# Modulation sums by block transposes and row sums on VectorE, folded by four small products, in place of TensorE transposes

## The reference

```python
c_act = jax.nn.silu(c)                       # 1 x 1024
for l in range(2):
    mod = c_act @ w_ada[l] + b_ada[l]        # 1 x 6144
    sh1, sc1, g1, sh2, sc2, g2 = jnp.split(mod, 6, axis=-1)
    h = rmsnorm(x, norm1[l]) * (1.0 + sc1) + sh1
    ...                                      # retention, pooling, gates from h @ w_in[l]
    x = x + g1 * (merged @ w_out[l])
    h2 = rmsnorm(x, norm2[l]) * (1.0 + sc2) + sh2
    gate, up = jnp.split(h2 @ w_ffn_in[l], 2, axis=-1)
    x = x + g2 * ((jax.nn.silu(gate) * up) @ w_ffn_out[l])
```

## Time and profile before

| | |
|---|---|
| median of 3 runs | 1407.83 us (1406.99 to 1409.58) |
| the profiled execution, its own time | 1406.93 us |
| its span, first to last instruction | 1405.1 us |
| TensorE (PE), matmuls | 1388.5 us busy, 99% |
| TensorE, weight loads (PEld) | 1306.0 us, 93% |
| VectorE (DVE) | 1117.1 us, 79% |
| ScalarE (ACT) | 845.7 us, 60% |
| GpSimd (POOL) | 101.3 us, 7% |
| mean granted TensorE clock | 0.998 |
| DMA, mean | 214 GB/s |

### The profile page before, as it was taken

The page is one execution under the profiler, slowest core; times in us unless marked ns, Lnnn a source line. Parts: engine busy times, 40 slices in busy tenths (PEclk is TensorE's granted clock), DMA queues, the critical chain, the costliest instruction groups (busy, mean ns, idle before and its releaser), DMA issues.

```text
span 1405.1 us, 25824 instructions
## 1 busy us (share of the span) xinstructions
PE 1388.5 (99%) x10437; PEld 1306.0 (93%) x10437; DVE 1117.1 (79%) x1690; ACT 845.7 (60%) x1307; POOL 101.3 (7%) x157
## 2 busy tenths in 40 slices
PE   8999999999999999999999999999999999999998
PEld 7898888899889888899999999998999999999987
DVE  7898988889898888888777788777677777876653
ACT  6776776345776875347576575554465764754452
POOL 2000111100000011103100000000031000000000
PEclk9999999999999999999999999999999999999999
DMA  9643999986545999979954588887699555777662
GB/s 256 171 143 97 285 272 277 297 226 179 145 137 157 299 267 288 299 205 257 312 150 147 172 239 237 242 246 219 181 265 305 150 151 179 237 217 229 189 184 72
DMA packets 472981, 301.34 MB, mean 214 GB/s; under 512 B 15116, under 2 KB 454416, under 8 KB 472736
## 3 DMA queue, kind: packets, MB, share of 16 engines
q1 hardware_dynamic: 455344, 239.57, 61.0%
q0 software_dynamic: 16704, 58.29, 12.7%
q10 hardware_dynamic: 816, 1.84, 0.4%
HBM read 289.43 MB, written 1.05 MB: 207 GB/s over the span
## 4 chain that ended last, share of the span: by engine, by line
PE 89%; DVE 6%; ACT 2%; issue 2%; DMA 1%; SPq 0%; ACTq 0%; DVEq 0%
PE acc L2107 14%; PE acc L2108 14%; PE acc L2109 14%; PE mx L2124 11%; PE mx L2125 6%; PE acc L2124 6%; PE acc L2125 3%; DVE w_lo L1180 2%; PE mx L2108 2%; PE mx L2107 2%; PE mx L2109 2%; DVE ada_acc L1270 1%; PE acc L2152 1%; PE acc L2154 1%; PE acc L2153 1%
## 5 line engine op out<-in xcount | busy, mean ns | idle before, releaser
L1180 DVE TENSOR_TENSOR w_lo<-raw,w_hi 128x1024 fp32r<-128x1024 f32 x450 | 542.8, 1220 | 127.4 <-ACT w_hi L591 125.0
L591 ACT ACTIVATE w_hi<-raw 128x1024 fp32r<-128x1024 f32 x450 | 465.3, 1052 | 137.4 <-DMA raw<-in_w_in 61.9
L2107 PE MATMUL acc<-h,w_hi 128*128 128x256 f32 (+1 forms) x1472 | 421.5, 286 | 2.9 <-DVE w_lo L1180 2.5
L2108 PE MATMUL acc<-h,w_hi 128*128 128x256 f32 (+1 forms) x1472 | 412.9, 280 | 0.0
L2109 PE MATMUL acc<-h,w_lo 128*128 128x256 f32 (+1 forms) x1472 | 411.5, 280 | 0.0
L2107 PEld LDWEIGHTS acc<-h,w_hi 128*128 128x128 f32 x1472 | 277.4, 188 | 9.0 <-issue 3.7
L2108 PEld LDWEIGHTS acc<-h,w_hi 128*128 128x128 f32 x1472 | 277.5, 189 | 2.6 <-issue 2.4
L2109 PEld LDWEIGHTS acc<-h,w_lo 128*128 128x128 f32 x1472 | 277.9, 189 | 0.0
L2124 PE MATMUL mx<-u,w_hi 128*128 128x512 f32 x756 | 264.4, 392 | 0.0
L2125 PE MATMUL mx<-u,w_lo 128*128 128x256 f32 x756 | 213.1, 282 | 0.0
L2124 PEld LDWEIGHTS mx<-u,w_hi 128*128 128x128 f32 x756 | 141.9, 188 | 29.2
(11 more groups left out here) (334 smaller groups left out, 2288.1 us busy)
## 6 DMA issues: line engine op xcount, KB each, us to landing
raw<-in_w_in SPq DMA_DIRECT2D x132, 512.0 KB, 4.2
ada<-in_w_ada POOLq DMA_DIRECT2D x96, 512.0 KB, 5.8
raw<-in_w_ffn_in SPq DMA_DIRECT2D x88, 512.0 KB, 4.5
raw<-in_w_up SPq DMA_DIRECT2D x64, 512.0 KB, 5.5
raw<-in_w_down SPq DMA_DIRECT2D x64, 512.0 KB, 5.8
raw<-in_w_out SPq DMA_DIRECT2D x32, 512.0 KB, 4.0
raw<-in_w_ffn_out SPq DMA_DIRECT2D x32, 512.0 KB, 4.1
raw<-in_w_ret_o SPq DMA_DIRECT2D x16, 512.0 KB, 4.1
```

Of the source, the lines that this page charges most:

```text
L591: nc.scalar.activation(w_hi[:, n % NS], raw[:, n % NS], ACT.Copy).then_inc(hi_ready, 1)
L1180: V.tensor_tensor(w_lo[:, n % NS], raw[:, n % NS], w_hi[:, n % NS].bitcast(F32), ALU.subtract).then_inc(lo_ready, 1)
L2107: mm(outp, w_hi[:, i % NS, k], rhs[:, k, 0], start=k == 0, stop=False)
L2108: mm(outp, w_hi[:, i % NS, k], rhs[:, k, 1], start=False, stop=False)
```

## The change

- The four TensorE transposes per group go, and with them `ada_part` and VectorE's row sum and bias add per group.
- A group's products now all go to the first half of `ada_acc`. Right behind the last of them VectorE transposes that half in blocks of 32x32 into the second half (`ada_turned`), and sums each block's rows: 128x512 become 128x16 in `ada_rows`. So partition 32a+k holds, for piece n of 128 columns and block m, the sum over the 32 partitions of block a for column 128n+32m+k.
- The sum over the four values of a is left. `ada_fold` (128x32, four identities of 32 one above the other) does it on TensorE: `ada_sums(n)` is now four products, one per m, each with 32 output partitions and 4 columns per group, for all groups of one place at once. The places (`ADA_FOLDS`, first group and count): groups 0 to 6 beside slab 8 of layer 1's up projection, 7 to 15 in the first retention stage where the transposes of group 15 stood, 16 to 21 in the second retention stage where those of group 21 stood, 22 and 23 beside slab 39 of the last FFN stage. `ada_columns(n)` is one add of the bias there. The groups of layer 0's MLP stage are folded only in the MLP stage of layer 1.
- `ada_fold` is made by one row sum on VectorE in `rest_of_vectors`, at the start.
- A product that starts a group now waits for the row sum of the group before (`ada_row`); `ada_turned` waits for its products and, from the second fold's groups on, for the fold before. `ADA_DONE` and the wait in `whole_tiles` follow.
- The loads stay on POOL's queue, in the same order with the same waits.

```diff
@@ -119,14 +119,10 @@
     return beside
 
 
-def ada_sums_at(stage, later):
-
-    g0, n, at = ADA_PLAN[stage]
-    return {at(8 * i + 7) + later: g0 + i for i in range(n)}
-
-
-
-ADA_DONE = (0, 0, 7, 7, 14, 16, 20, 22, 24)
+
+ADA_FOLDS = ((0, 7), (7, 9), (16, 6), (22, 2))
+FOLD_A, FOLD_F = 8, 39
+ADA_DONE = (0, 0, 0, 0, 7, 16, 16, 22, 24)
 
 
 TILE_NORMS = (2, 4, 5, 6, 7, 8)
@@ -247,13 +243,14 @@
         negsink = sb("negsink", [P, 12])
         cact = sb("cact", [P, KT])
         head_eps = sb("head_eps", [P, 1])
-        ada_part = sb("ada_part", [P, 4])
+        ada_fold = sb("ada_fold", [P, 32])
+        ada_rows = sb("ada_rows", [P, 9, 4, 4])
         few = sb("few", [P, 16])
         mean_eps = sb("mean_eps", [P, 1])
         wgrp = sb("wgrp", [P, LAYERS * 4, P])
 
 
-        sb("before_u2", [P, 32])
+        sb("before_u2", [P, 116])
         with ExitStack() as mlp:
             u2 = sb("u2", [P, MLP_UP, 2, S], F32R, mlp)
             ru = sb("ru", [P, 2, 2 * S], F32, mlp)
@@ -938,7 +935,8 @@
                 def whole_tiles(*tiles):
                     for k in tiles:
                         if k == 0:
-                            act.wait_ge(ada_out, (14, 20)[l])
+                            act.wait_ge(ada_row, (14, 20)[l])
+                            act.wait_ge(ada_out, (7, 16)[l])
                         normed_high(h_norm, 2 * l, k, [t.rearrange("p (c t) -> p c t", c=2) for t in (sqb, rb)], y2,
                                     nx_of(l), lambda k: mod_of(l, k))
 
@@ -1252,15 +1250,15 @@
 
                 e, part = divmod(q, 2)
                 g, k = divmod(q, 8)
-                o = ada_acc[:, g % 2]
+                o = ada_acc[:, 0]
                 if q == 0:
                     dve.wait_ge(c_silu, 1)
                 if part == 0:
                     dve.wait_ge(ada_landed[e % 3], 16 * (e // 3) + 16)
                 w = cact[:, k:k + 1]
                 if k == 0:
-                    if g >= 2:
-                        dve.wait_ge(ada_col, g - 1)
+                    if g >= 1:
+                        dve.wait_ge(ada_row, g)
                     ins = V.tensor_scalar(o, ada[:, e % 3, 0], w, None, ALU.mult)
                 else:
                     if part == 0:
@@ -1273,20 +1271,34 @@
                 else:
                     ca.done(ins)
 
-            def ada_columns(g):
-                dve.wait_ge(ada_col, g + 1)
-                ca.link(V.tensor_reduce(ada_part[:], mx[:, 0].rearrange("p (n k) -> p n k", n=4), AX, ALU.add))
-                V.tensor_tensor(modT[:, 4 * g:4 * g + 4], ada_part[:], vecT[:, V_BADA + 4 * g:V_BADA + 4 * g + 4],
-                                ALU.add).then_inc(ada_out, 1)
+            def ada_turned(g):
+
+                n = [at <= g < at + count for at, count in ADA_FOLDS].index(True)
+                dve.wait_ge(ada_sum, ADA_UNITS * (g + 1))
+                if n:
+                    dve.wait_ge(ada_col, n)
+                ca.link(V.transpose(ada_acc[:, 1], ada_acc[:, 0]))
+                V.tensor_reduce(ada_rows[:, g - ADA_FOLDS[n][0]].rearrange("p n m -> p (n m)"),
+                                ada_acc[:, 1].rearrange("p (b k) -> p b k", b=16), AX, ALU.add).then_inc(ada_row, 1)
+
+            def ada_columns(n):
+                at, count = ADA_FOLDS[n]
+                dve.wait_ge(ada_col, n + 1)
+                V.tensor_tensor(modT[:, 4 * at:4 * (at + count)], mx[:, 0, 0:4 * count],
+                                vecT[:, V_BADA + 4 * at:V_BADA + 4 * (at + count)], ALU.add).then_inc(ada_out, count)
 
             def beside(stage):
-                tiles, columns = ada_tiles(stage), ada_sums_at(stage, 6)
+                tiles = ada_tiles(stage)
 
                 def work(p):
                     for q in tiles.get(p, ()):
                         ada_product(q)
-                    if p in columns:
-                        ada_columns(columns[p])
+                        if q % 8 == 7:
+                            ada_turned(q // 8)
+                    if (*stage, p) == ("A", 1, FOLD_A + 2):
+                        ada_columns(0)
+                    if (*stage, p) == ("F", 1, FOLD_F + 2):
+                        ada_columns(3)
                 return work
 
             def scaled_pair(counts, n, b):
@@ -1321,6 +1333,7 @@
 
             def rest_of_vectors():
                 dve.wait_ge(boot_t, 6)
+                boot.done(V.tensor_reduce(ada_fold[:], ident.rearrange("p (a k) -> p k a", a=4), AX, ALU.add))
                 boot.done(V.tensor_scalar(vecT[:, V_LN2:V_C], acc[:, 3, V_LN2:V_C], float(D) ** 0.5, None, ALU.mult))
                 V.tensor_copy(vecT[:, V_C:P], acc[:, 3, V_C:P]).then_inc(vec_ready, 1)
                 boot.done(V.tensor_copy(vecT[:, P:V_MLN], acc[:, 3, P:V_MLN]))
@@ -1875,13 +1888,13 @@
                 lo_upto(p0 + 25)
                 ada_product(8 * g0 + 7)
                 lo_upto(p0 + 26)
+                ada_turned(g0)
                 ada_product(8 * g0 + 8)
                 ada_product(8 * g0 + 9)
                 lo_upto(p0 + 28)
                 ada_product(8 * g0 + 10)
                 ada_product(8 * g0 + 11)
                 lo_upto(p0 + 29)
-                ada_columns(g0 + 0)
                 ada_product(8 * g0 + 12)
                 lo_upto(p0 + 30)
                 ada_product(8 * g0 + 13)
@@ -1892,11 +1905,12 @@
                 pooled(0)
                 lo_upto(p0 + 32)
                 ada_product(8 * g0 + 15)
+                ada_turned(g0 + 1)
                 lo_upto(p0 + 33)
                 gated(0)
                 pooled(1)
                 lo_upto(p0 + 35)
-                ada_columns(g0 + 1)
+                ada_columns(1 + l)
                 gated_low(0)
                 pooled(2)
                 lo_upto(p0 + 36)
@@ -2164,12 +2178,12 @@
                     mm(mx[:, 0, 0:S], one, ssq[:, 0], start=True, stop=False)
                     mm(mx[:, 0, 0:S], one, ssq[:, 1], start=False, stop=True).then_inc(n_ss, 1)
 
-            def ada_sums(g):
-                pe.wait_ge(ada_sum, ADA_UNITS * (g + 1))
-                if g >= 1:
-                    pe.wait_ge(ada_out, g)
-                for n in range(4):
-                    ins = nc.tensor.transpose(mx[:, 0, n * P:(n + 1) * P], ada_acc[:, g % 2, n * P:(n + 1) * P], ident)
+            def ada_sums(n):
+
+                at, count = ADA_FOLDS[n]
+                pe.wait_ge(ada_row, at + count)
+                for m in range(4):
+                    ins = mm(mx[32 * m:32 * (m + 1), 0, 0:4 * count], ada_fold[:], ada_rows[:, 0:count, :, m], start=True, stop=True)
                 ins.then_inc(ada_col, 1)
 
             h_part = lambda k: hd2[:, k]
@@ -2488,11 +2502,9 @@
                 norm_sum(l * 2 + 1)
                 up_slab(2)
                 up_slab(3)
-                sums = ada_sums_at(("A", l), 4)
-
                 def ada_after(p):
-                    if p in sums:
-                        ada_sums(sums[p])
+                    if (l, p) == (1, FOLD_A):
+                        ada_sums(0)
 
                 pe.wait_ge(n_var, l * 2 + 2)
                 for k in range(MLP_UP):
@@ -2640,19 +2652,16 @@
                 pe.wait_ge(b_vsb, l * 4 + 1)
                 values2(2)
                 project(22, 23, 24)
-                pe.wait_ge(b_p, l * 8 + 1)
-                ada_sums(g0 + 0)
                 project(25)
                 pe.wait_ge(b_vsb, l * 4 + 3)
                 ret_outputs(0)
-                pe.wait_ge(ada_out, g0 + 1)
                 ret_scores(1)
                 project(26)
                 pe.wait_ge(b_vsb, l * 4 + 2)
                 ret_sums(0)
                 project(27, 28, 29, 30)
                 pe.wait_ge(b_p, l * 8 + 3)
-                ada_sums(g0 + 1)
+                ada_sums(1 + l)
                 pe.wait_ge(b_gt, l * 4 + 1)
                 ret_outputs(1)
                 project(31)
@@ -2708,11 +2717,9 @@
                 out_slab(6)
                 out_slab(7)
 
-                sums = ada_sums_at(("F", l), 4)
-
                 def ada_after(p):
-                    if p in sums:
-                        ada_sums(sums[p])
+                    if (l, p) == (1, FOLD_F):
+                        ada_sums(3)
 
                 for s in range(FFN_IN):
                     if s < 4:
```

More of the change, by code:

```diff
@@ L357, in program @@
         ada_landed = [sem(f"ada_landed{j}") for j in range(3)]
-        ada_sum = sem("ada_sum"); ada_col = sem("ada_col"); ada_out = sem("ada_out")
+        ada_sum = sem("ada_sum"); ada_row = sem("ada_row"); ada_col = sem("ada_col"); ada_out = sem("ada_out")
         s_con = sem("s_con"); s_con2 = sem("s_con2"); s_x = [sem(f"s_x{n}") for n in range(2)]
```

## The result

The change takes 1409.29 us (median of 20 runs, 1407.79 to 1413.52) where the kernel before, in runs beside it, takes 1407.24: 1.0016 times as long, 95% interval 1.001 to 1.0023, or 2.3 us slower (1.4 to 3.2); the two medians are 2.1 us apart. The prediction was 3.0 us slower. Every set of experiments had its own runs of the kernel before, and a ratio is against these: their medians are 1406.93 us beside e0, e1, e3 and e4, 1407.00 beside e5 to e8, 1406.58 beside e9 and e10, 1407.92 beside e11. A difference between experiments is one of medians where nothing else is said.

The account below looks back on a forecast made before the run. Both MLP stages were taken to end in a tie, VectorE's circle already later, with TensorE setting the rest. 2.4 + 3.0 - 2.6 + 0.2 = +3.0 us on 1406.93, stated as 1410.8 for the median, range 1405.5 to 1416.5.

Parts of the forecast that it names:

- The bound: Both MLP stages end in a tie of TensorE's work and VectorE's circle, the circle later; TensorE alone paces the others.
- VectorE's circle: VectorE and ScalarE waiting on each other's tiles in the MLP down projections, up to the boundary; forecast 3.3 us longer.
- the waits of 0.15 and 0.59 us: TensorE's weight loads waiting for the last h tile at the layer 0 and 1 boundaries; forecast to reach some 3 us.
- A group on VectorE: Block transpose and row sum per group: 1.46 us against 0.80, so 0.66 us more; 0.44 to 1.19 at the ends.
- Rival 2: The block transpose on VectorE takes two passes: 10 x 0.53 us more, 1416.1; chance 0.12.
- The MLP stages: Boundary shifts from five groups in each circle and earlier starts: +2.4 us in layer 0, +3.0 in layer 1.
- A fold: Four small fp32 products on TensorE, eight instructions: 0.6 us each, between 0.3 and 1.2.
- the part behind boundary 1: Retention and FFN stages, TensorE's: ten bursts give -4.4 us, three folds +1.8, together -2.6.
- The clock: Rival: TensorE's wait at a boundary drops its clock to 1.2 GHz, 1.7 us each time: 1412.5 or 1414.2; chance 0.18.
- The sum: All stages together: 2.4 + 3.0 - 2.6 + 0.2 = +3.0 us on the profiled 1406.93; 1410.8 stated for the median.
- rival 1: The circle has room for VectorE's added work, so TensorE sets both MLP stages: 8.0 us faster, 1399.8; chance 0.13.
- The start: One more row sum on VectorE at the kernel's start, where its copies stand on the chain: +0.2 us.

Follow-up runs that it names:

- e0: The change run again unaltered, for a second profile: 1409.07 us, ratio 1.0014 to the kernel before.
- e1: The change with groups 0 to 13 (MLP stages) summed as before and the new sums for the rest: 1403.47 us, ratio 0.9975 to the kernel before.
- e3: The change with the block transposes of groups 0 to 13 left out (times only): 1400.41 us, ratio 0.9955 to the kernel before.
- e4: The change with the block transposes of groups 0 to 13 done twice: 1416.81 us, ratio 1.0072 to the kernel before.
- e5: The change with the block transposes of groups 14 to 23 (retention and FFN stages) done twice: 1409.48 us, ratio 1.0014 to the kernel before.
- e8: The change with the four products of each fold done four times over: 1410.72 us, ratio 1.0032 to the kernel before.
- e9: The change with nine unused fp32 products on TensorE before its wait for the last h tile at both MLP boundaries: 1412.96 us, ratio 1.0043 to the kernel before.
- e10: e6 with every block transpose done twice: 1399.78 us, ratio 0.9952 to the kernel before.
- e11: As e9, with four products in place of nine: 1408.02 us, ratio 1.0004 to the kernel before.
- e7: The kernel before with one group moved from each MLP stage to layer 0's FFN stage: 1405.73 us, ratio 0.9986 to the kernel before.
- e6: The change with one group moved from each MLP stage to layer 0's FFN stage, five folds: 1396.63 us, ratio 0.9925 to the kernel before.

## Why the prediction was right, point by point

- **The bound.** Right. The two MLP stages end when VectorE's circle ends (e3, e4), the others are TensorE's (e5). That VectorE's 15 us of idle time in a stretch of 93 are no room is shown by e4: 3.7 us more of work per circle came out as 3.3 and 3.8 us of time. That it was a tie, with VectorE already the later one, is shown from the other side by e7: with a lighter circle the waits of 0.15 and 0.59 us vanish.
- **A group on VectorE.** The block transpose was taken at 0.70 us, between bounds of 0.48 and 1.23, and is 0.71; the group at 1.46, and is 1.47. The choice of the row of a two-source operation carried it; no row of before showed a block transpose, so that it fits to 0.01 us is in part luck. The estimate from the Trainium skill (VectorE: DVE Perf Modes, The three transpose paths, and Vector Engine (DVE) Microarchitecture Reference, The reshape front-end and per-opcode configuration) was 0.71, and the trace agrees with it at this one width. Rival 2, two passes, is out.
- **The MLP stages.** Forecast +2.4 and +3.0, measured +2.7 and +2.8 (e0). VectorE's circle in layer 1, from its last wait for ScalarE's copy of a bank to the boundary, grew from 104.4 us (523.23 to 627.66) to 107.7 (525.76 to 633.45), 3.3 as forecast. TensorE's wait in layer 1 was right in its sum, 6.1 us forecast and seen, and less so in its split: some 3 us were forecast in one piece on the boundary, and it was 2.3, with 3.8 on late low parts.
- **A fold.** Forecast 0.6 us, between 0.3 and 1.2, measured 0.41: 17 ns for each instruction, and the larger part once per fold. The lower end was the better reading. Three folds make 0.6 us, and account for the part behind boundary 1: -2.6 forecast, -3.2 to -3.5 measured where the clock does not fall.
- **The clock.** The mechanism was named, the chance mis-sized. I gave the fall 0.18, as a rival with 1.7 us per boundary, and left it out of the sum; it was seen in each of the five profiles with a wait of 2.3 us at both boundaries and nothing in its place, behind one boundary each, at 1.1 to 1.4 us.
- **The sum.** Its closeness is in part luck. Four folds were taken 0.2 us too dear each, 0.8 in all, and the fall left out costs 1.1 to 1.4. With the folds at their price the sum is 2.3, with the fall as seen 3.4 to 3.7. From the first mark on, e0 is 2.9 over the profile before (2.74 - 0.26 + 2.77 - 2.35), and the runs say 2.3 (1.4 to 3.2). By the prediction's own bar of 0.2% the result is "same", to which it gave 0.28, and not "slower", to which it gave 0.56. One figure under rival 1 is wrong: with boundaries at -0.88 and at -0.88 + 0.6, the sum changes sign where 0.54 of each 3.3 us reaches the boundary, not 0.4.
- **The start.** +0.2 forecast, not to be told from the spread of the profiles (142.3 to 143.8 us to the first mark).
- **Rival 1**, room in the circle, fell with e0, e3 and e4. It is what e6 makes true by another plan: its gain of 8.0 us, and 2.4 more, is there once the circle has room.

## What to carry to other kernels

Where two engines end a stage in a tile-by-tile circle, the idle time of the busier one inside the circle is not room for more work; look whether it ever waits for the engine that is to be relieved. Work taken off one of two tied engines and put on the other costs its full price there and gains nothing here, in that stage; in another stage of the same kernel the same edit is free. So move it together with the plan that says where such work stands: the plan alone brought some 1 to 2 us, the sums alone lost 2.3, both brought 10.4.

## What the runs showed of the hardware that was not expected

- In five profiles of five with TensorE waiting 2.3 us at both boundaries and for late low parts ahead of them, the granted clock fell to the 1.2 GHz level behind one boundary, never both. With products in the wait it did not (e9, e11, one profile each). A single wait of 2.24 us without late low parts was followed by a fall in one place (1066.7 us in the first profile of the change), one of 2.26 us in e3 was not.
- Small fp32 products with 32 output partitions follow each other at 17 ns per instruction, while the entry into them costs 0.08 us once, on top of what a burst of whole transposes had (e0, e8).
- An fp32 product of 128x256 took two instructions of some 0.22 us (17 in 3.83 us, e9) at a granted clock of 1.00, where one of the kernel's rounded products takes 0.12 from start to start.
